# One VectorE instruction and two low parts moved at the first FFN step, all final norms of a block in the next block's second step

## What is computed

```
def conv_ffn(xn, prev, w_up, conv_w, w_down):
    u = xn @ w_up
    uc, new = causal_dwconv(u, prev, conv_w)
    a, g = jnp.split(uc, 2, axis=-1)
    return (jax.nn.silu(g) * a) @ w_down, new
...
        x = x + y                                   # after the mixer
        y, f = conv_ffn(rmsnorm(x, norm2[l]), ffn_s[l], w_up[l], ffn_conv_w[l], w_down[l])
        x = x + y
...
    return rmsnorm(x, final_norm), ...
```

## Time and profile before

| | us |
|---|---|
| three runs: median (lowest to highest) | 2320.63 (2320.24 to 2322.08) |
| the profiled execution, its own time | 2318.33 |
| span of its instructions | 2316.4 |
| PE busy | 2246.0 (97%) |
| DVE busy | 1718.1 (74%) |
| POOL busy | 1204.9 (52%) |
| ACT busy | 1007.2 (43%) |

### The profile page before, as it was taken

One profiled execution on the slowest core, in us unless ns is written; L12 is line 12 of the kernel. 1 busy time (PEld: TensorE's weight loads), 2 busy tenths in 40 slices (PEclk: granted clock), 3 DMA queues, 4 the chain that ended last, 5 costly groups with the idle time before them and its releaser, 6 DMA issues. The chain is left out here.

```text
span 2316.4 us, 39569 instructions
## 1 busy us (share of the span) xinstructions
PE 2246.0 (97%) x12585; PEld 2063.6 (89%) x12585; DVE 1718.1 (74%) x2534; ACT 1007.2 (43%) x1968; POOL 1204.9 (52%) x1245
## 2 busy tenths in 40 slices
PE   7999999999999998999999999999999988999998
PEld 6998889998889977999999988999999987999997
DVE  6578775477655777898988987767666687788877
ACT  4544463343534454434444445333333346444344
POOL 3654723225333458777778774444444454554552
PEclk9999999999999999999999999999999999999999
DMA  4653556544376667444444467444444447556563
GB/s 128 195 173 133 183 180 212 166 134 158 132 259 202 224 213 266 160 163 164 156 171 156 171 227 254 150 145 149 145 149 146 154 160 266 194 187 202 183 203 111
DMA packets 265749, 412.79 MB, mean 178 GB/s; under 512 B 15198, under 2 KB 188147, under 8 KB 265651
## 3 DMA queue, kind: packets, MB, share of 16 engines
q1 hardware_dynamic: 265651, 411.51, 52.7%
HBM read 313.31 MB, written 98.16 MB: 178 GB/s over the span
## 5 line engine op out<-in xcount | busy, mean ns | idle before, releaser
L1690 PE MATMUL ps<-xo,wq 128*128 128x384 f32 (+1 forms) x1848 | 599.6, 324 | 17.0 <-issue 4.6
L1691 PE MATMUL ps<-xo,wq 128*128 128x384 f32 (+1 forms) x1848 | 598.5, 324 | 0.0
L1692 PE MATMUL ps<-xo,wq 128*128 128x384 f32 (+1 forms) x1848 | 598.0, 324 | 0.0
L2566 DVE TENSOR_TENSOR resid<-resid,ps 128x512 f32<-128x512 f32 (+1 forms) x728 | 477.5, 681 | 74.9 <-PE ps L1692 44.9
L1027 POOL TENSOR_TENSOR wq<-wu_raw,wq 128x256 fp32r<-128x256 f32 x396 | 388.0, 1002 | 97.5 <-ACT wq L1150 97.5
L1690 PEld LDWEIGHTS ps<-xo,wq 128*128 128x128 f32 x1848 | 350.4, 190 | 39.5 <-issue 14.8
L1691 PEld LDWEIGHTS ps<-xo,wq 128*128 128x128 f32 x1848 | 351.1, 190 | 20.2
L1692 PEld LDWEIGHTS ps<-xo,wq 128*128 128x128 f32 x1848 | 351.3, 190 | 0.0
L2583 DVE SCALAR_TENSOR_TENSOR up_y<-up_u,params,up_y 128x768 f32<-128x768 f32 (+1 forms) x260 | 283.2, 1089 | 46.5 <-ACT up_y L1194 27.0
L536 POOL TENSOR_TENSOR wq<-wu_raw,wq 128x256 fp32r<-128x256 f32 x174 | 145.5, 858 | 288.7 <-ACT wq L1276 288.7
L1690 PE MATMUL ps<-wd_hi,hid_hi 128*128 128x512 f32 x704 | 276.3, 392 | 13.0 <-DVE resid L2566 10.3
(11 more groups left out here) (262 smaller groups left out, 4234.2 us busy)
## 6 DMA issues: line engine op xcount, KB each, us to landing
wq<-w_ops SPq DMA_DIRECT2D x176, 512.0 KB, 4.5
wu_raw<-in_w_up_dram SPq DMA_DIRECT2D x89, 512.0 KB, 4.1
w_ops<-wq SPq DMA_DIRECT2D x88, 512.0 KB, 2.6
wq<-m_ops SPq DMA_DIRECT2D x80, 512.0 KB, 3.8
wd_raw<-in_w_down_dram SPq DMA_DIRECT2D x66, 512.0 KB, 5.2
wu_raw<-in_w_in_dram SPq DMA_DIRECT2D x40, 512.0 KB, 4.9
m_ops<-wq SPq DMA_DIRECT2D x40, 512.0 KB, 3.1
x_in<-in_x_prompt_dram SPq DMA_DIRECT2D x32, 512.0 KB, 5.6
```

The lines of the kernel that those rows point to most:

```text
L1690: pe.matmul(out, lh, rh, start=(first and n == 0), stop=False, skip_group_check=skip)
L1691: pe.matmul(out, ll, rh, start=False, stop=False, skip_group_check=skip)
L1692: last = pe.matmul(out, lh, rl, start=False, stop=end, skip_group_check=skip)
L2566: last = dve.tensor_tensor(resid[0:m, t, s], resid[0:m, t, s], ps[0:m, bank, :], ALU.add)
```

## The change

Three edits, none of which alters a value:
1. First FFN step: the low part of weight operand 5 moves from POOL to DVE, as one 128x512 instruction between the last two scalings of the second norm; PE and SP wait for the fourth POOL count and for DVE's. POOL takes operand 6 next (which waits for DVE's instruction and counts two). DVE takes the low part of data operand 5 after `r_2` and that of operand 6 after `r_3`; ACT's load of silu's table goes behind its copy of data operand 6.
2. Final norms of tiles 0 and 1: from the end of a block's first step into its second step, on ACT in front of `high_hidden` with the table load, on DVE after `r_2`; tile 2's scaling after the next additions, tile 3's after `r_3`. Two table loads fewer for each block.
3. SP: stores and reloads of tiles 0 and 1 at i = 1, of 2 and 3 at i = 3, of 4 and 5 at i = 4. `FIRST_ROWS` becomes 3, 3, 2, so that the first addition waits for three reloads in block 1 and for two in block 2.

```diff
-FIRST_ROWS = [3, 4, 4]
+FIRST_ROWS = [3, 3, 2]
...
+        FIRST_LOW_V = pair_lows(NB * NPAIR - 1, NP - 1)[0] + 1
+        def first_low_up(eng):
+            eng.wait_ge(wu_lo, splits(0, 0, 4))
+            eng.wait_ge(pair_low_v, FIRST_LOW_V)
...
-                    sp.wait_ge(wu_lo, splits(0, 0, 5))
+                    first_low_up(sp)
                     load_up(0, 1)
...
-                    if edge == 1 and b and i in (1, 3):
-                        results(b, range(i + 1, min(i + 3, TILES[b - 1])))
+                    if edge == 1 and b and i in (1, 3, 4):
+                        first_tile = {1: 0, 3: 2, 4: 4}[i]
+                        results(b, range(first_tile, min(first_tile + 2, TILES[b - 1])))
...
-                if edge == 0 and b:
-                    results(b, range(2))
...
-            for i in range(NP):
+            for i in range(5):
                 low_up(0, 0, i)
+            pool.wait_ge(pair_low_v, FIRST_LOW_V)
+            low_up(0, 0, 6, 2)
...
-            act.preload_act_table(ACT.Silu)
             high_x(0, 5)
...
+                if edge == 1 and b:
+                    act.preload_act_table_set("natural_log_exp_and_others")
+                    final_rstd(b - 1, 0)
+                    final_rstd(b - 1, 1)
                 if prev:
                     high_hidden(*prev, 1 - par)
...
                 if edge == 1 and b:
-                    act.preload_act_table_set("natural_log_exp_and_others")
                     final_rstd(b - 1, 2)
                     final_rstd(b - 1, 3)
...
                     high_x(b, 6 if first_of_all else 5)
+                if first_of_all:
+                    act.preload_act_table(ACT.Silu)
...
-                if edge == 0 and b:
-                    act.preload_act_table_set("natural_log_exp_and_others")
-                    for t in range(2):
-                        final_rstd(b - 1, t)
-                    act.preload_act_table(ACT.Silu)
...
+                if not nxt:
+                    dve.wait_ge(wu_hi, HIGHS + splits(0, 0, 5))
+                    at, w = WQ_AT[5], wu_source(5)
+                    dve.tensor_tensor(wq[:, at, 1], w, wq[:, at, 0].bitcast(F32), ALU.subtract).then_inc(pair_low_v, 1)
...
                 if edge == 1 and b:
+                    final_scale(b - 1, 0)
+                    final_scale(b - 1, 1)
+                adds(1)
+                if edge == 1 and b:
                     final_scale(b - 1, 2)
-                    final_scale(b - 1, 3)
-                adds(1)
+                if first_of_all:
+                    low_x(0, 5)
...
+                if edge == 1 and b:
+                    final_scale(b - 1, 3)
                 adds(3)
                 if edge == 0:
-                    low_x(b, 5)
+                    low_x(b, 6 if first_of_all else 5)
...
-                if edge == 0 and b:
-                    for t in range(2):
-                        final_scale(b - 1, t)
```

More of the change, by code:

```diff
@@ L1018, in _, with low_up @@
                         pool.memset(t[:, :, BTS[b] + GAP + DEC:ncol], 0.0).then_inc(gap_zero, 1)
-            def low_up(b, f, i):
+            def low_up(b, f, i, count=1):
                 if i not in SPLIT[b]:
@@ L1027, in low_up @@
                     last = pool.tensor_tensor(wq[:, WQ_AT[i], 1, r], src[:, r], wq[:, WQ_AT[i], 0, r].bitcast(F32), ALU.subtract)
-                last.then_inc(wu_lo, 1)
+                last.then_inc(wu_lo, count)
             def low_x(b, i):
@@ L2003, in ffn_step @@
                 for i in range(NP):
-                    if i in SPLIT[b]:
+                    if b == 0 and edge == 0 and i == 5:
+                        first_low_up(pe)
+                    elif i in SPLIT[b]:
                         pe.wait_ge(wu_lo, splits(b, f, i))
@@ L2672, in ffn_step @@
                 adds(4)
-                if edge == 0:
+                if edge == 0 and b:
                     low_x(b, 6)
```

## The result

The changed kernel takes 2332.64 us (median of 5 runs, 2330.51 to 2333.83); the kernel before, run beside it, 2322.08 us (5 runs, 2320.24 to 2324.11). The ratio is 1.0050, with an interval of 1.0039 to 1.0062: slower by about half a percent. The forecast was 2325.8 us in a range that ended at 2329.6, so the direction came true and the size did not. The two profiled executions differ by 14.1 us of span (2330.5 against 2316.4): 0.42 us lie ahead of the ConvFFN, where the change does nothing, 0.16 in its start, 4.35 in block 1 and 9.2 in block 2. The medians differ by 10.6 us only: the profiled execution of the kernel before (2318.33 us) was 3.8 us faster than the median beside which the change was measured, so about 3.5 of the 14.1 us are scatter from one execution to the next.

A forecast was written before the change was run, and what follows sets the result against it. TensorE, busy 97% of the span, was taken as the bound, so only its idle gaps counted. Start -1.65, block 1 +2.0 and block 2 +4.8 gave +5.15 us on 2320.63: 2325.8 us, range 2320.3 to 2329.6.

The forecast's parts named there:

- The mechanism and its places: Second steps of blocks 1 and 2: moved norms wait for stores, SP's stores stand behind weights, `c21` late; +2.0 and +4.8 us.
- The start: Start of the ConvFFN, block 0's first step: weight sums begin 1.7 us earlier, worth -1.65 us.
- from -0.5 to -3.3: Range for the ConvFFN's start: -0.5 if ACT's or GpSimd's queue takes over, -3.3 if the clock's fall also goes.
- Block 1, the step that failed: Block 1's second step: assumed store and reload landings of 5 to 6.1 us make `c21` 5.7 us late; block total +2.0 us.
- the 1.6 us of clock: Block 1, after the group at 1435.22: the half-clock stretch paid in full should go, -1.65 us.
- Block 2, the same term and an analogy: Block 2's second step: weight copy 1.5 us late as in block 1, store 3 landing in 5.7 us, `c21` +4.8 us.
- tile 2 is the late one: Block 1's first residual addition: `FIRST_ROWS` 3 asks one tile less, but still waits for tile 2's reload.
- 5.4 us later: Block 1, SP's queue: tile 2's reload issued at 1419.5, so the first addition starts at 1425.6 instead of 1420.17.
- short landings: Rival, chance 0.16: stores land in about 3 us; block 1 about -1, block 2 about +2; 2320 to 2321 us.
- the rule behind it: DMA cost of about 2.0 us plus bytes / 436 GB/s; each round 2 to 3 us shorter, sum about 0.
- heavier: Rival, chance 0.16: landings near 6.9 us and clock falls where PE bounds; block 1 +5, block 2 +6, start -1.

The follow-up runs named there:

- The two cures: Changed kernel with stores of tiles 2 and 3 ahead of the weight load (0.9993), or weight copies ahead of norms 2 and 3 (1.0005); both together 0.9992.
- the single edit: Kernel before with only SP's order changed: stores and reloads of tiles 2 and 3 behind the weight loads, tiles 4 and 5 at i = 4; 2333.70 us, ratio 1.0058.
- The first edit alone: Kernel before with only the change's edit to the first FFN step; 2316.45 us, ratio 0.9989.
- the best kernel: Kernel before with the change's first FFN step edit and FIRST_ROWS at 3, 3, 2, norms and stores in their old order; 2312.67 us, ratio 0.9975.

## Why the prediction was wrong in size

- **The mechanism and its places were right.** The second step's stores behind the weight wait, the long gap ahead of a down group, `c21` held by the last scales in both blocks, and no wait for rows in block 2: all stand in the trace after. The two cures and the single edit show that this mechanism, not another, makes the loss.
- **The start.** The product at 890.92 was to come 1.65 us sooner; it came 1.8 us sooner (1.35, and the 0.42 us that the kernel was behind). But the bound "from -0.5 to -3.3" held the clock's fall behind `r_3` fixed or gone. It became longer: 6.8 us at 0.50 in 902.70 to 909.50, and the stage ends 0.16 us late. The sum also followed the chain to that one product alone. In the next step the weight sums, which hold `r_3`, started only 0.3 us sooner, because they waited for a weight load. The first edit alone, with a fall of 3.4 us, gained 1.1 us in this stage.
- **Block 1, the step that failed: the landing times.** I took 5.0 us for tile 1's store, 6.1 for the reload of tile 2 and 6 for tile 3's store. They took 5.5, 6.9 and 7.8. Tile 3's store alone makes 1.8 of the 2.2 us by which `c21` was missed. In SP's queue it stands 2.0 us behind the weight load, with 2 MB issued between (the weight load, a weight operand, a store and a reload). The prediction saw the 2 MB and took "about 6 us" for them, from rows whose longest landing was 6.9. The weight copy was to be 1.7 us late and was 1.9 (1414.71 against 1412.25, less 0.58), so that step held. `c21` was +7.9 instead of +5.7, and the group that was at 1435.22 came +5.9 instead of +3.6. From that go the 1.6 us of clock, which were saved as forecast: +4.35 against +2.0.
- **Block 2, the same term and an analogy.** "By analogy the weight copy is 1.5 us late" was 2.9: 1935.75 against 1927.97, less 4.9 brought along. There tile 1's store took 6.7 us (1927.42 to 1934.13). From tile 3's store (1941.85) to its norm (1950.28) are 8.4 us, and the sum had 5.7. Together they make +9.2 instead of +4.8 (1.4 us from the copy, 2.7 from tile 3's store). The upper bound of 6.9 us, the longest landing of the earlier trace rows, was no bound: the longest now are longer.
- **The row counts.** The prediction gave the smaller count no value in block 1, since "tile 2 is the late one". The runs price the counts at 4 us in the old order and at about 7 in the new. The wait of the earlier trace rows at 1420.17 ended with the fourth reload, that of tile 3 (1414.08). The sum took the delay of tile 2's reload from that time, "5.4 us later", although tile 2's own had gone out at 1412.48. The value of the smaller count was in this way mixed into the delay and never named. In the sum it could not matter, because the last scales came later than the addition; with four reloads the addition comes last (1429.00). This error hid a part of the other: without the counts the change would have cost 18 us.
- **The rival "short landings" and the rule behind it.** The range's low end rested on 3 us a landing. The changed kernel's least is 3.6 us in block 1 (the landing times above). The estimate of 3.2 us rests on the Trainium skill, page "DMA: Bandwidth & Descriptors", section "Anatomy of one DMA — SWDGE (gpsimd) path". It gives the two costs of one DMA, as a fit to DMAs that GpSimd issues; here SP issues them. The trace comes near it only for a store with nothing issued in the 5 us ahead (2.9 us in the earlier trace rows), and the stores that decide here took 5.5 to 8.4 us.
- **The rival "heavier"** (2329 to 2331 us, 0.16) had the right cause and was still too low: it bounded the landings by 6.9 us.

What stays open is how much of each gain or loss is the clock's. Its falls differ from kernel to kernel (none in the two late stretches of the best kernel, 6 to 14 us at half clock in one piece in the slower ones), and no run here changed the falls alone.

## What to carry to other kernels

Where an edit moves a DMA behind others on its queue, do not price its landing by the median of the trace: add up what will stand ahead of it, and do not take the longest landing seen as the end of the range (6.9 us before, 8.4 us after, here). Ahead of a queued wait put whatever is ready sooner and is waited for sooner; here a finished tile stood 6.6 us (scaled by 1413.3, issued at 1419.89) behind a weight load that could come later at no visible cost, and one move in the program gave 13 us. When an edit bundles several parts, price each on the chip by itself: two of this one's parts gain about 6 us together, and the third hid them.

## What the runs showed of the hardware

- A 512 KB store landed after 2.9 us when nothing had been issued in the 5 us ahead of it, after 6.3 us with 1 MB issued in the 1.05 us ahead, and after 7.8 and 8.4 us with 2 MB in the 2 us ahead. A 64 KB store with 1 MB ahead still took 4.6 us. The reload that VectorE's addition waits for, 512 KB, took 6.1 us in the old place and 6.9 to 8.4 us in the new one.
- TensorE's granted clock stood at 0.50 (1.2 of the two levels 1.2 and 2.4 GHz) behind gaps of 1.80 us as behind those of 9.52 us, but not for the same time: about 3.3 us behind the short ones of the kernel before, 6.7 us around the 7.64 us gap, 10.2 us around that of 9.52 and 13 us around one of 10.38 us (with the row counts put back). After a gap of 2.99 us it fell, after one of 2.00 and one of 1.71 us in the same place it did not.
